# Two ends of an up-projection stage in another order on four engines

## The reference, cut to what matters

```python
x = layer_norm(alpha * x + m, ln_mix_g[i], ln_mix_b[i])      # m: the mixer's output
u = x @ w_up                                                # (512, 1024) @ (1024, 2 * 2816)
c = conv_b + sum(conv_w[j] * shifted(u, j) for j in 0..2)   # causal, per channel
g, val = c[:, :2816], c[:, 2816:]
f = (silu(g) * val) @ w_down                                # (512, 2816) @ (2816, 1024)
x = layer_norm(alpha * x + f, ln_ffn_g[i], ln_ffn_b[i])
```

## Time and profile before

| | us |
|---|---|
| median of three runs (lowest, highest) | 1231.78 (1230.88, 1231.8) |
| the profiled execution | 1231.07 |
| its span, first to last instruction | 1229.3 |
| PE busy in it | 1191.5 (97%) |
| DVE / ACT / POOL busy | 735.9 / 628.5 / 678.7 |

### The profile page before, as it was taken

One profiled execution on the slowest core, in us unless ns is written; L12 is line 12 of the kernel. 1 busy time (PEld: TensorE's weight loads), 2 busy tenths in 40 slices (PEclk: granted clock), 3 DMA queues, 4 the chain that ended last, 5 costly groups with the idle time before them and its releaser, 6 DMA issues.

```text
span 1229.3 us, 20284 instructions
## 1 busy us (share of the span) xinstructions
PE 1191.5 (97%) x7714; PEld 1052.3 (86%) x7714; DVE 735.9 (60%) x1368; ACT 628.5 (51%) x1089; POOL 678.7 (55%) x418
## 2 busy tenths in 40 slices
PE   9999999998999999899999999999899999999997
PEld 9877777787999999888888788878899999987885
DVE  2045656358988888612280355654999888872126
ACT  3245555445766666512342466753566666652223
POOL 4543535255877777655534333334577777765453
PEclk9999999999999999999999999999999999999999
DMA  7321212131233323322232212122123222232311
GB/s 290 112 86 61 91 63 94 36 104 35 103 107 107 111 107 110 128 97 89 103 109 99 78 60 68 69 69 103 35 93 114 103 103 103 102 137 103 102 68 69
DMA packets 20041, 117.44 MB, mean 96 GB/s; under 512 B 2448, under 2 KB 2832, under 8 KB 7568
## 3 DMA queue, kind: packets, MB, share of 16 engines
q1 hardware_dynamic: 18400, 112.21, 25.8%
q10 hardware_dynamic: 1584, 4.51, 1.1%
HBM read 110.41 MB, written 2.10 MB: 92 GB/s over the span
## 4 chain that ended last, share of the span: by engine, by line
PE 82%; DVE 8%; ACT 4%; POOL 3%; issue 2%; DVEq 0%; ACTq 0%; POOLq 0%
PE bank L1480 32%; PE bank L1181 28%; PE bank L1212 13%; POOL w_lo L302 2%; PE bank L1264 2%; PE bank L1291 1%; PE bank L1350 1%; PE bank L1329 1%; ACT w_hi L400 1%; PE bank L1278 1%; DVE x L824 1%; DVE a_lo L1115 1%; PE bank L1156 1%; DVE ln_mul L801 1%; PE bank L1339 1%
## 5 line engine op out<-in xcount | busy, mean ns | idle before, releaser
L302 POOL TENSOR_TENSOR w_lo<-w_raw,w_hi 128x1024 fp32r<-128x1024 f32 x116 | 297.2, 2584 | 370.0 <-ACT w_hi L400 359.8
L400 ACT ACTIVATE w_hi<-w_raw 128x2048 fp32r<-128x2048 f32 x55 | 105.2, 1912 | 208.7 <-PE bank L1181 200.7
L1480 PE MATMUL bank<-t_hi,w_hi 128*128 128x256 f32 x640 | 181.4, 283 | 2.9 <-POOL w_lo L361 2.9
L1480 PE MATMUL bank<-t_hi,w_lo 128*128 128x256 f32 x640 | 181.1, 283 | 0.0
L1480 PE MATMUL bank<-t_lo,w_hi 128*128 128x256 f32 x640 | 181.1, 283 | 0.0
L361 POOL TENSOR_TENSOR w_lo<-w_raw,w_hi 128x512 fp32r<-128x512 f32 x120 | 156.9, 1308 | 20.6 <-ACT w_hi L612 19.8
L1181 PE MATMUL bank<-w_hi,a_hi 128*128 128x512 f32 x480 | 153.3, 394 | 9.6 <-DVE a_lo L1115 6.8
L1181 PE MATMUL bank<-w_hi,a_lo 128*128 128x512 f32 x480 | 152.0, 391 | 0.0
L1181 PE MATMUL bank<-w_lo,a_hi 128*128 128x512 f32 x480 | 151.7, 391 | 0.0
L1212 PE MATMUL bank<-xt_hi,w_hi 128*128 128x512 f32 (+1 forms) x416 | 148.1, 356 | 2.4 <-ACT v_all L430 1.7
L1212 PE MATMUL bank<-xt_lo,w_hi 128*128 128x512 f32 (+1 forms) x416 | 148.5, 357 | 0.0
(11 more groups left out here) (129 smaller groups left out, 2518.6 us busy)
## 6 DMA issues: line engine op xcount, KB each, us to landing
w_raw<-w_stream SPq DMA_DIRECT2D x97, 1024.0 KB, 4.8
x<-x_in SPq DMA_DIRECT2D x4, 512.0 KB, 7.5
gain<-ln_in ACTq DMA_DIRECT2D x4, 512.0 KB, 4.1
shift<-ln_in ACTq DMA_DIRECT2D x4, 512.0 KB, 5.1
qs<-qc SPq DMA_DIRECT2D x16, 128.0 KB, 2.0
ks<-kc SPq DMA_DIRECT2D x16, 128.0 KB, 2.0
out<-x SPq DMA_DIRECT2D x3, 512.0 KB, 2.6
w_raw<-w_stream SPq DMA_DIRECT2D x2, 512.0 KB, 6.3
```

The costliest lines, as they stand in the source:

```text
L302: pool.tensor_tensor(w_lo[slot(c)][:, part], w_raw[s][:, part], w_hi[slot(c)][:, part].bitcast(F32), ALU.subtract).then_inc(lo_ready, 1)
L400: act.activation(w_hi[slot(c)][:, :], w_raw[c % 2][:, :], ACT.Copy).then_inc(hi_ready, 2)
L1480: mm = pe.matmul(out, lhs[s][:, at], rhs[:, k, :], start=(k, v) == (0, 0), stop=(k, v) == (3, 2))
```

## The change

Nothing is computed differently, and no instruction is added or left out. Four engines get another order at both ends of the up stage, in both layers:

- **POOL, entry:** the token sums wait until all four tiles of the LayerNorm are out. The rest of the first `W11` moves ahead of the token rests.
- **ACT, entry:** the Silu table and the head of the first `W11` move between `xt_heads` of token tile 2 and of token tile 3.
- **DVE, entry:** `first_sums` of the first body moves ahead of the token rests and of the taps of tile 0.
- **ACT, exit:** `chunk_heads(0)` and `chunk_heads(1)` follow each half of the first down chunk's heads; the second down chunk's heads move ahead of the last gate, and the gain and shift transfers behind it.
- **DVE, exit:** `chunk_rests(0)` moves ahead of the last `values_combined`.

```diff
@@ -368,14 +368,17 @@
+                pool.wait_ge(N[2 * l]["xn"], NT)
                 token_sum(0)
                 token_sum(1)
+                w_rest(0, W11, w_raw[(b + AT_UP + FIRST) % 2][:, 0:Q])
                 for j in range(2):
                     t_rest(T3, j, 4 * j + 1)
                     t_rest(T4, j, 4 * j + 4)
                 for m in range(NW):
                     raw = w_raw[(b + AT_UP + FIRST + m) % 2]
-                    w_rest(m, W11, raw[:, 0:Q])
+                    if m:
+                        w_rest(m, W11, raw[:, 0:Q])
@@ -641,8 +644,9 @@
                             if not first:
                                 keep_first(m - 1, again)
                                 freed(m, W11)
-                            act.wait_ge(raw_full[(b + AT_UP + FIRST + c) % 2], filled(b + AT_UP + FIRST + c, it))
-                            w_head(W11, raw[:, 0:Q])
+                            if not first:
+                                act.wait_ge(raw_full[(b + AT_UP + FIRST + c) % 2], filled(b + AT_UP + FIRST + c, it))
+                                w_head(W11, raw[:, 0:Q])
@@ -677,7 +681,6 @@
-                        act.preload_act_table(ACT.Silu)
                         act.wait_ge(conv_full, 16)
@@ -711,18 +714,17 @@
                             act.activation(w_hi[slot(down_first)][:, part], w_raw[down_first % 2][:, part],
                                            ACT.Copy).then_inc(hi_ready, 1)
-                        chunk_heads(0, used=False)
+                            chunk_heads(g, used=False)
                         value_combined(last, 1)
+                        act.wait_ge(w_used, down_first)
+                        heads(down_first + 1, used=False)
+                        gate_combined(last, 1)
                         act.wait_ge(*w.at("lo_p", 5 * NW))
                         load_gain(i)
-                        gate_combined(last, 1)
                         silu(KF - 1, 1)
-                        act.wait_ge(w_used, down_first)
-                        heads(down_first + 1, used=False)
 
 
                         act.preload_act_table_set("natural_log_exp_and_others")
-                        chunk_heads(1, used=False)
                         chunk_heads(2)
@@ -754,6 +756,13 @@
                         xt_heads(i + 1, 2)
+                        if i % 2 == 0:
+                            act.preload_act_table(ACT.Silu)
+                            first = after + FIRST
+                            s, part = operand(l, W11)
+                            act.wait_ge(raw_full[first % 2], filled(first, 0))
+                            act.wait_ge(w_used, after)
+                            act.activation(w_hi[s][:, part], w_raw[first % 2][:, 0:Q], ACT.Copy).then_inc(w["hi"], 1)
                         xt_heads(i + 1, 3)
@@ -1099,7 +1108,8 @@
-                    first_sums(m, c, it, level > 1)
+                    if level > 0:
+                        first_sums(m, c, it, level > 1)
                     second_sum(m, c)
@@ -1118,6 +1128,7 @@
                 dve.wait_ge(conv_full, 16)
                 tokens_mixed(0)
                 tokens_mixed(1)
+                first_sums(0, 0, 0, False)
@@ -1134,8 +1145,8 @@
                 early_products(last)
+                chunk_rests(0)
                 values_combined(last, 1)
-                chunk_rests(0)
                 value_taps(KF - 1, 1)
```

## The result

The changed kernel took 1213.11 us (median of 4 runs, 1212.87 to 1213.52) against 1231.39 us before: a ratio of 0.9852, 95% interval 0.9835 to 0.9869, or 18.3 us less where 17.4 was forecast. The span of the profiled execution fell by 17.8 us, from 1229.3 to 1211.5.

What follows compares the result with a forecast made beforehand. PE was taken to bound the kernel, its time following its idle stretches. Entries of 11.5 us and exits of 5.9 us sum to 17.4 us less, giving a median of 1214.4 us, range 1209.8 to 1219.5.

Steps and rivals of the forecast that it cites:

- The LayerNorm's tail was held up by the token sums: Layer entry, last token tile: with POOL's token sums moved behind, DVE's two slow instructions take 0.19 and 1.28 us, 4.2 earlier.
- The clock: Transposes at layer entry: without the 4.3 us idle, nothing lowers PE's clock from 2.4 to 1.2 GHz.
- Table load and `W11` head at no cost: Layer entry on ACT: both fit in its 9.09 us idle time; without that cover they would cost 1.9 us.
- Two lost turns at the sums: Layer entry on DVE: worst case taken, two waits for POOL around the early weight sums, taps at 295.7 (best 293.9).
- the new wait at `SUM_2`: First body of the up stage: PE waits 1.6 us for `SUM_2`'s rest, where no stall was before.
- The exit: Up stage to down stage: PE's waits for DVE's first down-chunk rests go, 2.95 us gained a layer, 5.9 in both.
- The stall at the second chunk's weights: Second down chunk: POOL's second weight rest comes late and holds PE for about 0.25 us.
- The pace of the bodies: Up stage: bodies stay at 10.1 us; a slower rival had them fall to DVE's pace, 1270 us, chance 0.02.
- the two entries: Start of each layer's up stage: 5.9 us gained in layer 0 and 5.65 in layer 1, 11.5 together.
- the first (no lost turns): Rival at the entry: DVE gets both sums between POOL's instructions, no stall at `SUM_2`, 1210.5 to 1211 us, chance 0.2.

Runs made afterwards that it cites:

- the half exit: The changed kernel with only the first down chunk's operand heads and rests kept early at the exit, ACT's later work in the former order: 1219.88 us.

## Why the prediction was right

1. **The LayerNorm's tail was held up by the token sums.** Right to the hundredth: 0.16 and 1.28 us, and shown both ways by adding and removing the wait alone. Taken out of the changed kernel it cost 10.2 us; alone on the kernel before it gave 8.5, since there the clock took 1.5 us back in one layer. The prediction prices the entry as a whole and has no term for this edit alone.
2. **The clock.** Right: 1.00 from 282 to 284 and transposes at 1.09 us.
3. **Table load and `W11` head at no cost.** Right: done at 281.15, 2.1 us before the transposes' result. Their old place costs 3.1 us, not the 2.4 expected of that run: the expectation left out that POOL's `W11` rest would meet DVE's last token rest.
4. **Two lost turns at the sums.** Right in kind and nearly in size. Transposes to taps were forecast as 14.04 us (281.66 to 295.7) and took 13.81 (282.11 to 295.92). From taps to `SUM_2`'s rest 5.67 were forecast, and 5.66 measured. The term that was mis-sized is the new wait at `SUM_2`: 1.6 forecast, 1.27 and 1.30 measured, so each entry gained 0.2 us more than worked out, 6.1 and 5.9 for 5.9 and 5.65. (By its own figures, 4.2 for 4.3 and 1.3 for 1.6, layer 1 should have had 0.4 us less than layer 0, not 0.25. Measured were 0.27, so the slip did no harm, which is luck.)
5. **The exit.** Right: DVE had its turn between POOL's two rests (2.91 us from 496.75, while POOL's two took 5.78 for 4.77), and both waits went. Its sum holds small errors that partly cancel. It starts the down stage at 506.35, but the gap to close was larger: from the last up matmul's start to the first down one's were 1.92 us before (506.01 to 507.93), and are 0.12 now (500.33 to 500.45), so 1.8 us went and not 1.6. It has POOL's second rest of the first chunk out at 507.6, just ahead of PE's 507.7; its own rows give 507.8 (501.83 + 4.77, and 1.24 for DVE's turn), and so it came: POOL ended at 501.92 and PE took up that half at 501.98, 0.14 us behind its pace. The stall at the second chunk's weights was forecast as 0.25 and was 0.1 (513.14, POOL out at 513.08). So an exit gave 3.1 for 2.95. That the first half is worth little without the second is shown by the half exit.
6. **The pace of the bodies.** Right: 101 us for ten bodies on PE, DVE 89.85 against 89.79.

Four terms, the two entries and the two exits, each 0.15 to 0.25 us larger, make the 0.8 us by which the gain of 18.2 exceeds 17.4. Of the rivals, none took the place of the forecast; the first (no lost turns) fell with the 2.72 us of the two sums.

The Trainium skill, "SBUF — State Buffer", section "Who interferes with whom", also says that a DVE instruction with at most one SBUF input, outside the 2-port performance modes, does not contend with GpSimd. By that rule this trace agrees: the pair of token rests at 281.98, one input in PSUM, took 1.28 us under a token sum, as the same pair did before, at 285.76 with POOL idle.

## What to carry to other kernels

When a tiny instruction takes as long as a neighbour's large one, look at what the other engine ran: moving work that nobody waits for out from under a critical tail gave about half of this gain (8.5 us alone, 10.2 with the other edits, of 18.3). An edit that moves an instruction earlier has to be priced with what it will run beside there, and it may come out at nothing, as the weight sums did. And a wait removed from a chain counts only up to the next late link, so price the two together before doing one, as the half exit shows.

## What was not expected of the hardware

PE's clock fell to 1.2 GHz once after an idle time of only 2.25 us (it was low from 302 to 305 us, and 1.5 us were lost), while the same 2.25 us in the other layer, and 2.75 and 2.81 us at the exit (the stretches behind them show 1.00), left it at 2.4 GHz; after 4.2 and 4.3 us, in both layers of the kernel before, it fell. So an idle time of this length has a price that one trace doesn't settle. What decides it is not shown by these runs.
